# Row maxima of an attention stage: how they reach the query rows as extra contraction rows

## The chip, the cores and the metric

The kernel runs on one core of one Trainium2 chip. The metric is the device time of the whole kernel in microseconds (us), the median of several runs. One execution was also recorded by the hardware profiler; all start times below are us from the start of its span. The engines are called PE (TensorE), DVE (VectorE), ACT (ScalarE), POOL (GpSimd) and SP (SyncE, which issues DMAs). PEld is PE's loading of weights. "L1268" is line 1268 of the kernel before.

## The reference, cut to what matters

One layer of a hybrid encoder on 1024 tokens of width 1024 in float32: RMS norm, one combined projection, attention with 8 heads beside a convolution branch, gates, an output projection, and a mixture of 32 experts. The change touches the attention alone:

```python
# q, k: (1024, 8 heads, 96), v: (1024, 8 heads, 64); tokens are grouped in chunks of 64
s = einsum('bqhd,bkhd->bhqk', q, k) * scale
mask = key_chunk <= query_chunk          # a query sees its own chunk and all earlier ones
p = softmax(where(mask, s, -inf), axis=-1)
out = einsum('bhqk,bkhd->bqhd', p, v)
```

## The kernel before, in words

**Stages.** The projection units fill the first 340 us. The last of their epilogue and the opening of the attention lie at 340 to 374 us, the attention proper at 374 to 567 us, the branch projections up to about 654 us, the output projection with the router up to about 770 us, and the experts after that.

**The attention's items.** There are 16 items n, head h = n % 8 and group G = n // 8: group 0 holds queries 0 to 511 (4 key tiles of 128 keys), group 1 queries 512 to 1023 (8 key tiles). PE computes the scores twice. First it computes them with queries on partitions (`max_scores`, L1730), only so that DVE can take each query's maximum over its keys (L1218). Then it computes them transposed, with keys on partitions (`scores_T`, L1791 to L1793), so that ACT can take the exponential (`exps`, L908) and PE can multiply by the values (`pv`, L1804).

**How maximum and mask enter the transposed scores.** The query operand `qT` has 96 data rows and 12 further rows, and the key operand `kT` too (XK = 96 + 12 = 108 rows). Rows 96 to 103 carry the mask: a key column has -1e30 in the row of its own tile where the key lies in the tile's second chunk, and the query column has 1 in that row where the query lies in the tile's first chunk. Rows 104 to 107 subtract the maximum: the keys have four rows of ones, and the query columns have the negated maximum of query tile i in row 104 + i and zeros in the other three.

**The step in question, "mT".** DVE writes the negated maxima of an item as four columns of a small tile `nmax` [128 queries, 108] whose columns 96 to 103 are ones. PE transposes `nmax` into a PSUM bank (L1714, one transpose of 128 columns, output 108 x 128). DVE then multiplies rows 96 to 107 of that, repeated over the four query tiles, by a constant mask `own_tile` and writes the 12 x 512 result into `qT` (L1268):

```python
v.tensor_tensor(qT[t % 3][0][rows, :]..., M[rows, 0:P]...broadcast_to([XK - QK, GT, P]),
                own_tile[t // HEADS][rows, :, :], ALU.mult).then_inc(m_free[b], 1)
```

There are 16 such steps, mT(0) to mT(15). `scores_T` of an item waits for the semaphore `m_free` that this step increments.

**The order of the work.** Each engine's order is written out by hand. `OPENING` lists the work before the first transposed score (mT(0) is in it). Then, for each item n and key tile k, every engine walks the same list `slots(n, k)` of small jobs ("misc"): PE issues `scores_T(x + 2)`, the jobs, `pv(x)`; ACT issues `exps(x + 2)`, its part of the jobs and, at an item's last tile, two copies of sums and values out of PSUM (L941, L942); DVE does its part of the jobs and the reciprocals of the sums (L1352). In group 0 mT(n + 1) stands first in the slot k = 0; in group 1 it stands in the slot k = 2. The other jobs are the pieces of `max_scores` for item n + 2, the transpose of the queries (`qT`: PE L1709, ACT L845, DVE L1263), and in group 0 the preparation of tokens 512 to 1023 (q0, q1, kv0, kv1, kT0, kT1, ks). All jobs that need a PSUM bank take turns in two banks, and PE's next job in a bank waits for the `m_free` of the last one.

POOL fills the constants: `nmax`'s ones at the start (L608 to L610), `key_pad` and `own_tile` before the attention (L641 to L650). Every `qT` buffer gets its rows from 96 on from `own_tile` once (`mask_rows`, L671).

Of the kernel before, what the change touches and what calls it, by code (L numbers as in the profile page):

```python
# [26 lines left out]
ALU = mybir.AluOpType  # L27
ACT = mybir.ActivationFunctionType
AX = mybir.AxisListType

P = 128
D = 1024
T = 1024
NTILE = T // P
KD = D // P
HEADS, NOPE, ROPE, VD = 8, 64, 32, 64
QK = NOPE + ROPE
# [10 lines left out]
CHUNK = 64  # L48
# [13 lines left out]
TAPS_PER_UNIT = 7  # L62
LO_SPLIT = 5
LN_UNIT = 20
LN_SPLIT = (6, 11, 15, 19)
RUN = 4


def build(nc, x, positions, g_mix, w_in, g_q_lora, w_uq, g_kv_lora, w_ukv, g_qk_q, g_qk_k,
# [4 lines left out]
    base = (nc.sbuf_base + 127) // 128 * 128  # L74
# [11 lines left out]
    def small(name, shape, dt=F32):  # L86
        n = 2 if dt == BF16 else 4
        for s in shape[1:]:
            n *= s
        return place(name, shape, dt, room(n))  # L90
# [30 lines left out]
    qT = [[place(f"qT_{n}{r}", [P, CW], F32R, o + 2 * K * s) for s, n in enumerate(("hi", "lo"))] for r, o in enumerate(q_at)]  # L121
    qn = [place(f"qn{t}", [P, HEADS, QK], F32, o) for t, o in enumerate(
        (R2 + 56 * K, R2 + 8 * K, R2 + 11 * K, R3 + 29 * K, R6 + 12 * K, R6 + 16 * K, R2, R2 + 3 * K))]
    XK = QK + 12
    kn = [place(f"kn{i}", [P, HEADS, XK], F32, R2 + o) for i, o in enumerate((59 * K, 16 * K, 22 * K + 512, 26 * K))]
    sq2 = place("sq2", [P, HEADS, QK], F32, R2 + 19 * K + 512)
    pT = place("pT", [P, 3, CW], F32, R2 + 22 * K + 512)
# [40 lines left out]
    qd = place("qd", [P, NTILE, DOWN], F32, QDO)  # L168
# [33 lines left out]
    rs1 = small("rs1", [P, NTILE])  # L202
    ss3 = small("ss3", [P, 3, NTILE])
    ssh = small("ssh", [P, 4, 2, HEADS])
    key_pad = small("key_pad", [P, NTILE, 12])
    nmax_a = small("nmax_a", [P, 4])
    nmax = [small(f"nmax{i}", [P, XK]) for i in range(2)]
    wr = place("wr", [P, KD, NG + NE], F32, R6)
    br = place("br", [P, NG + NE], F32, R6 + 2 * K)
    lg = place("lg", [P, NTILE, NG], F32, R6 + 3 * K)  # L210
# [63 lines left out]
    with ctx:  # L274
# [117 lines left out]
        def piece_at(n, i):  # L392
            return GT * n + i if n < HEADS else GT * HEADS + 2 * GT * (n - HEADS) + i
# [192 lines left out]
        def _(pool):  # L586
# [3 lines left out]
            def link(ins):  # L590
                n[0] += 1
                ins.then_inc(pch, 1)
                pool.wait_ge(pch, n[0])
# [11 lines left out]
            g.memset(ab[:, NTILE, :], 0.0)  # L605
            g.memset(one_row[:, :], 1.0)
            g.memset(zero_i[:, :], 0)
            for i in range(2):  # L608
                link(g.memset(nmax[i][:, :], 0.0))
                g.memset(nmax[i][:, QK:QK + NTILE], 1.0)  # L610
            link(g.memset(before[:, :], 0.0))

            g.affine_select(out=before[:, :], in_=before[:, :], compare_op=ALU.is_ge, fill=1.0, base=0,
# [25 lines left out]
            pool.wait_ge(conv_done, NC)  # L639
            g.memset(vv[:, :, :, VD:2 * VD], 1.0)  # L640
            link(g.memset(key_pad[:, :, :], 0.0))  # L641
            link(g.memset(key_pad[:, :, NTILE:NTILE + 4], 1.0))
            for t in range(NTILE):
                link(g.memset(key_pad[CHUNK:P, t, t:t + 1], MASKED))
            for G in range(2):
                link(g.memset(own_tile[G][:, :, :], 0.0))
                link(g.affine_select(out=own_tile[G][:, :, 0:CHUNK], in_=own_tile[G][:, :, 0:CHUNK], compare_op=ALU.not_equal, fill=1.0,
                                     base=-(QK + GT * G), pattern=[[-1, 4], [0, CHUNK]], channel_multiplier=1))
                g.affine_select(out=own_tile[G][:, :, :], in_=own_tile[G][:, :, :], compare_op=ALU.not_equal, fill=1.0,
                                base=-(QK + NTILE), pattern=[[-1, 4], [0, P]], channel_multiplier=1).then_inc(pad_ok, 1)  # L650

            def q_norm(t):
                s2 = ssh[:, t % 4, :, :]
# [102 lines left out]
        def _(act):  # L756
# [49 lines left out]


            def misc(kind, t):
                if kind[:2] in ("mx", "mT", "qd", "kd", "ks"):
                    return  # L810
                b, nth = place_of[kind, t]
                M = pb[:, MISC_BANK[b], :]
                act.wait_ge(m_full[b], nth + 1)
                h = 4 * (kind[-1] == "1")
                if kind in ("q0", "q1"):
                    if (kind, t) == ("q0", GT + 2):
                        for i in range(2):
                            act.wait_ge(gate_out[i], 16 * KD)
                    a.activation(qn[t][:, h:h + 4, :], M[:, 0:4 * QK].rearrange("p (h c) -> p h c", h=4), ACT.Copy).then_inc(m_free[b], 1)
                    if kind == "q1":  # L820
                        b0, nth0 = place_of["q0", t]
                        act.wait_ge(m_free[b0], nth0 + 1)
                        act.wait_ge(m_free[b], nth + 1)
                        if t:
                            act.wait_ge(head_ss, sums_of(kind, t))
                        a.activation(sq2[:, :, :], qn[t][:, :, :], ACT.Square).then_inc(qk_sq, 1)
                if kind in ("kv0", "kv1"):
                    kv = M.rearrange("p (h c) -> p h c", h=4)
                    k = kn_of(t)
                    if t == 0:  # L830
                        act.wait_ge(pad_ok, 2)
                    a.activation(k[:, h:h + 4, 0:NOPE], kv[:, :, 0:NOPE], ACT.Copy)
                    a.activation(vv[:, t, h // 2:h // 2 + 2, :].rearrange("p a (s c) -> p a s c", s=3)[:, :, 0::2, :],
                                 kv[:, :, NOPE:].rearrange("p (a s) c -> p a s c", s=2), ACT.Copy).then_inc(m_free[b], 1)
                    if kind == "kv1":
                        b0, nth0 = place_of["kv0", t]
                        act.wait_ge(m_free[b0], nth0 + 1)
                        act.wait_ge(m_free[b], nth + 1)
                        act.wait_ge(head_ss, sums_of(kind, t))
                        a.activation(sq2[:, :, 0:NOPE], k[:, :, 0:NOPE], ACT.Square).then_inc(qk_sq, 1)  # L840
                if kind in ("kT0", "kT1"):
                    a.activation(kT[0][0:XK, h:h + 4, t * P:(t + 1) * P], M[0:XK, :].rearrange("p (h t) -> p h t", h=4),
                                 ACT.Copy, scale=vcol[0:XK, V_NK:V_NK + 1]).then_inc(qk_hi, 1)
                if kind == "qT":
                    a.activation(qT[t % 3][0][0:QK, :], M[0:QK, :], ACT.Copy, scale=vcol[0:QK, V_NQ:V_NQ + 1]).then_inc(qk_hi, 1)  # L845

# [242 lines left out]
        def _(dve):  # L1089
# [120 lines left out]
            def misc(kind, t):  # L1210
                if kind[:2] == "mx":
                    i, G = int(kind[2]), t // HEADS
                    y = piece_at(t, i)
                    tile = i // 2 if G else i
                    w = CW if G and i % 2 == 0 else (tile + 1) * P
                    to = nmax_a[:, tile:tile + 1] if G and i % 2 == 0 else nmax[t % 2][:, QK + NTILE + tile:QK + NTILE + tile + 1]
                    dve.wait_ge(sc_ok, y + 1)
                    v.tensor_reduce(out=to, in_=pb[:, 2 * (y % 2), 0:w], axis=AX.X, op=ALU.max, negate=True).then_inc(mx_ok, 1)  # L1218
                    if G and i == 2 * GT - 1:
                        dve.wait_ge(mx_ok, y + 1)  # L1220
                        m = nmax[t % 2][:, QK + NTILE:XK]
                        v.tensor_tensor(m, m, nmax_a[:, :], ALU.min).then_inc(mxc_ok, 1)
                        dve.wait_ge(mxc_ok, t - HEADS + 1)
                    return
                s2 = ssh[:, t % 4, :, :]
                if kind == "ks":
                    k = kn_of(t)
                    if t == 0:
                        dve.wait_ge(tab_ok, 1)
                    dve.wait_ge(head_rs, t + 1)  # L1230
                    v.tensor_tensor(k[:, :, 0:NOPE], k[:, :, 0:NOPE], s2[:, 1, :].unsqueeze(2).broadcast_to([P, HEADS, NOPE]), ALU.mult)
                    v.tensor_copy(k[:, :, QK:XK], key_pad[:, t:t + 1, :].broadcast_to([P, HEADS, 12]))
                    v.tensor_tensor(k[:, :, NOPE:QK], krr[:, t:t + 1, :].broadcast_to([P, HEADS, ROPE]),
                                    s2[:, 1, :].unsqueeze(2).broadcast_to([P, HEADS, ROPE]), ALU.mult).then_inc(k_ok, 1)
                    return
# [24 lines left out]
                if kind == "qT":  # L1260
# [1 line left out]
                    hi, lo = qT[t % 3]  # L1262
                    v.scalar_tensor_tensor(out=lo[0:QK, :], in0=M[0:QK, :], scalar=vcol[0:QK, V_NQ:V_NQ + 1], in1=hi[0:QK, :].bitcast(F32),  # L1263
                                           op0=ALU.mult, op1=ALU.subtract).then_inc(m_free[b], 1)
                if kind == "mT":
                    rows = slice(QK, XK)
                    dve.wait_ge(m_full[b], nth + 1)
                    v.tensor_tensor(qT[t % 3][0][rows, :].rearrange("p (i t) -> p i t", i=GT), M[rows, 0:P].unsqueeze(1).broadcast_to([XK - QK, GT, P]),  # L1268
                                    own_tile[t // HEADS][rows, :, :], ALU.mult).then_inc(m_free[b], 1)


            unit_lo(0)
# [343 lines left out]
        def _(pe):  # L1616
# [53 lines left out]
            def misc(kind, t):  # L1670
# [39 lines left out]
                if kind == "mT":  # L1710
                    pe.wait_ge(mx_ok, piece_at(t + 1, 0))
                    if t >= HEADS:
                        pe.wait_ge(mxc_ok, t - HEADS + 1)
                    i = t_.transpose(M[0:XK, 0:P], nmax[t % 2][:, :], ident[:, :])  # L1714
                i.then_inc(m_full[b], 1)

            def max_scores(n, i):
# [314 lines left out]
```

## Time and profile before

| | us |
|---|---|
| runs shown: median (lowest, highest) of 3 | 1154.52 (1152.56, 1154.81) |
| the profiled execution's own time | 1160.95 |
| its span, first to last instruction | 1158.9 |
| PE busy in the span | 1084.1 (94%) |
| DVE busy | 863.4 (74%) |
| ACT busy | 580.6 (50%) |
| POOL busy | 326.7 (28%) |

The mean granted clock of TensorE over the span is 0.981 of full speed. The chain of waits that ended last is PE for 46% of the span, DVE for 6%, DMA for 6% and ACT for 2%. In the timelines a line gives the start of a group of instructions, the time from the first one's start to the last one's end, engine, line, operation, output and inputs, shapes and the count; in brackets stands the idle time of the engine just before, and what ended it. Matmuls overlap: the distance between two starts is what one costs PE, its own duration is longer.

### The profile page before, as it was taken

What the parts mean: (1) busy time and instruction counts of PE and PEld (TensorE: products, weight loads), DVE (VectorE), ACT (ScalarE), POOL (GpSimd) and SP (SyncE); (2) the same over time, 40 slices, a digit from 0 to 9 for tenths busy, and PEclk for the clock granted to TensorE, in tenths of its full rate; (3) what the DMA queues carried; (4) which work ended last, traced back from release to release, by engine and by line L of the source; (5) the groups of instructions that cost most, each with busy time, mean ns of one, the idle gap of its engine ahead of it and who ended that gap; (6) DMA issues with size and microseconds to landing.
All of it is one profiled execution on the core that took longest, in us unless ns stands there. A gap on an engine that the chain in (4) does not pass through costs nothing.

```text
span 1158.9 us, 15310 instructions
## 1 busy us (share of the span) xinstructions
PE 1084.1 (94%) x5117; PEld 872.7 (75%) x5117; DVE 863.4 (74%) x1095; ACT 580.6 (50%) x738; POOL 326.7 (28%) x323
## 2 busy tenths in 40 slices
PE   6999999999998887999999999988999999998896
PEld 6988888888764555666688888877788888886684
DVE  5438999998547567667456666676999999997894
ACT  5531211221547553445423222224888888887883
POOL 4010000002084450000000000012477777763653
PEclk8999999999999998999999999998999999999998
DMA  6021222333110001000592245465999989988972
GB/s 247 1 55 36 54 84 87 101 104 96 64 37 18 1 0 37 1 1 1 167 312 66 61 176 187 182 232 183 330 358 338 313 322 309 325 303 294 331 243 33
DMA packets 99108, 176.47 MB, mean 152 GB/s; under 512 B 12364, under 2 KB 62711, under 8 KB 99063
## 3 DMA queue, kind: packets, MB, share of 16 engines
q1 hardware_dynamic: 86262, 150.69, 37.6%
q0 software_dynamic: 10432, 16.81, 6.1%
q10 hardware_dynamic: 2368, 8.41, 1.8%
q8 instruction: 24, 0.39, 0.1%
q14 instruction: 22, 0.17, 0.1%
HBM read 161.18 MB, written 35.65 MB: 170 GB/s over the span
## 4 chain that ended last, share of the span: by engine, by line
PE 46%; DVE 6%; DMA 6%; ACT 2%; issue 1%; SPq 1%; ACTq 0%; POOL 0%; DVEq 0%; POOLq 0%
PE pb L1621 11%; PE pb L1623 11%; PE pb L1622 11%; PE pb L1804 4%; DMA wed_raw<-in_w_e_down 4%; PE pb L1949 2%; DMA wgu_raw<-in_w_e_up 2%; PE pb L1867 1%; PE pb L1792 1%; PE pb L1793 1%; PE pb L1791 1%; PE pb L1730 1%; ACT wgu_hi L1011 1%; DVE prob_sums L1352 1%; PE pb L1858 1%
## 5 line engine op out<-in xcount | busy, mean ns | idle before, releaser
L1546 DVE TENSOR_TENSOR wgu_lo<-wgu_raw,wgu_hi 128x2048 fp32r<-128x2048 f32 x72 | 164.9, 2292 | 32.1 <-ACT wgu_hi L1011 30.2
L1161 DVE SCALAR_TENSOR_TENSOR cv<-up,dwc,cv 128x1024 f32<-128x1024 f32 x120 | 154.1, 1284 | 3.7
L1621 PE MATMUL pb<-hT_hi,ws_hi 128*128 128x512 f32 x384 | 155.0, 404 | 1.7 <-ACT lnr L889 1.6
L1011 ACT ACTIVATE wgu_hi<-wgu_raw 128x2048 fp32r (+1 forms) x72 | 137.9, 1916 | 25.8 <-issue 10.7
L1623 PE MATMUL pb<-hT_hi,ws_lo 128*128 128x512 f32 x384 | 149.8, 390 | 0.0
L1622 PE MATMUL pb<-hT_lo,ws_hi 128*128 128x512 f32 x384 | 149.7, 390 | 0.0
L1621 PE MATMUL pb<-wgu_hi,hgT_hi 128*128 128x512 f32 x288 | 116.7, 405 | 5.2 <-DVE hgT_lo L1550 5.2
L1623 PE MATMUL pb<-wgu_hi,hgT_lo 128*128 128x512 f32 x288 | 112.9, 392 | 0.0
L1622 PE MATMUL pb<-wgu_lo,hgT_hi 128*128 128x512 f32 x288 | 112.7, 391 | 0.0
L733 POOL DMA_INDIRECT out<-yb,rcol x36 | 71.0, 1973 | 99.3 <-PE pb L1949 44.0
L625 POOL TENSOR_SCALAR rs<-ss 128x1 f32<-128x1 f32 x16 | 5.3, 330 | 311.0 <-ACT h2T L971 294.6
L1578 DVE TENSOR_TENSOR wed_lo<-wed_raw,wed_hi 128x1024 fp32r<-128x1024 f32 x70 | 82.4, 1218 | 6.8 <-ACT wed_hi L1020 6.8
L1621 PEld LDWEIGHTS pb<-hT_hi,ws_hi 128*128 128x128 f32 x384 | 72.3, 188 | 19.2 <-issue 3.5
L1622 PEld LDWEIGHTS pb<-hT_lo,ws_hi 128*128 128x128 f32 x384 | 72.3, 188 | 16.6 <-issue 1.5
L1623 PEld LDWEIGHTS pb<-hT_hi,ws_lo 128*128 128x128 f32 x384 | 72.2, 188 | 15.2
L908 ACT ACTIVATE pT<-pb 128x512 f32<-128x512 f32 (+1 forms) x96 | 46.6, 489 | 68.2 <-PE pb L1793 67.9
L1020 ACT ACTIVATE wed_hi<-wed_raw 128x1024 fp32r x70 | 70.4, 1054 | 19.7 <-PE pb L1623 9.9
L1804 PE MATMUL pb<-pT,vv 128*128 128x512 f32 (+1 forms) x192 | 79.9, 499 | 0.0
L805 ACT ACTIVATE ws_hi<-ws_raw 128x1024 fp32r<-128x1024 f32 x32 | 33.8, 1059 | 80.1 <-PE pb L1623 47.8
L857 ACT ACTIVATE gring<-pb,vcol 128x1024 f32<-128x1024 f32 x16 | 17.9, 1118 | 107.8 <-PE pb L1623 107.8
L715 POOL TENSOR_TENSOR icol<-stok,zero_i 128x1 int32<-128x1 int32 x34 | 65.7, 1934 | 17.0 <-PE pb L1949 17.0
L1621 PEld LDWEIGHTS pb<-wgu_hi,hgT_hi 128*128 128x128 f32 x288 | 54.3, 188 | 19.8 <-issue 8.9
(329 smaller groups left out, 2535.2 us busy)
## 6 DMA issues: line engine op xcount, KB each, us to landing
wgu_raw<-in_w_e_gate SPq DMA_DIRECT2D x32, 1024.0 KB, 7.5
wgu_raw<-in_w_e_up SPq DMA_DIRECT2D x32, 1024.0 KB, 17.8
wed_raw<-in_w_e_down SPq DMA_DIRECT2D x32, 1024.0 KB, 20.0
ws_raw<-in_w_in SPq DMA_DIRECT2D x24, 512.0 KB, 3.7
gates_kept<-gring ACTq DMA_DIRECT2D x16, 512.0 KB, 2.6
gates<-gates_kept SPq DMA_DIRECT2D x16, 512.0 KB, 7.4
xs<-in_x SPq DMA_DIRECT2D x8, 512.0 KB, 8.5
wout<-in_w_out SPq DMA_DIRECT2D x1, 4096.0 KB, 14.4
```

The source lines that it names most:

```text
L715: g.tensor_tensor(icol[b][:, :], stok[:, bass.ds(count - 1, 1)], zero_i[:, :], ALU.add).then_inc(ic_ok, 1)
L733: g.indirect_dma_start(out=out[0], out_offset=bass.IndirectOffsetOnAxis(ap=rcol[b][:, 0:1].bitcast(U32), axis=0), in_=yb[b][:, :], in_offs ...
L908: a.activation(pT[:, x % 3, c0:CW], pb[:, 4 + x % 2, c0:CW], ACT.Exp).then_inc(ex_ok, 1)
L1011: a.activation(wgu_hi[q % 2][:, :, ks, :], raw, ACT.Copy).then_inc(gu_hi, 1)
L1020: a.activation((end_hi if end else wed_hi)[:, h, :], wed_raw[:, bass.ds((e + (DSLOTS - 1)) % DSLOTS, 1), h, :].rearrange("p o f -> p (o f) ...
L1161: i = v.scalar_tensor_tensor(out=cv[:, c, :], in0=src, scalar=w, in1=cv[:, c, :], op0=ALU.mult, op1=ALU.add)
L1546: v.tensor_tensor(wgu_lo[q % 2][:, :, ks, :], wgu_raw[:, bass.ds((e + (SLOTS - 1)) % SLOTS, 1), :, ks, :].rearrange("p o g k f -> p (o g) ...
L1578: v.tensor_tensor((end_lo if end else wed_lo)[:, h, :], wed_raw[:, bass.ds((e + (DSLOTS - 1)) % DSLOTS, 1), h, :].rearrange("p o f -> p (o ...
L1621: t_.matmul(out, w(0), m(0), start=start, stop=False)
L1622: t_.matmul(out, w(0), m(1), start=False, stop=False)
L1623: return t_.matmul(out, w(1), m(0), start=False, stop=stop)
L1804: t_.matmul(pb[:, VALUE_BANK[n % 2], c0:CW], vv[:, k, h // 2, VD * (h % 2):VD * (h % 2) + 2 * VD], pT[:, x % 3, c0:CW], start=(k == 0), st ...
```

## The change

`nmax` becomes one tile [128, 2 groups, 2 buffers, 4 query tiles, 9 columns]. Columns 0 to 7 of a query tile's nine are the mask, constants that POOL writes once: 1 in the first 64 partitions in the column of that tile of that group. Column 8 is the tile's negated maximum, which DVE writes. PE multiplies each of the four [128, 9] blocks with the identity, an ordinary matmul and not the transpose form, into the four 128-column parts of rows 96 to 104 of the PSUM bank. ACT copies these 9 x 512 values into `qT`, where DVE multiplied. The keys need one row of ones in place of four, so XK goes from 108 to 105 rows, and the tiles and copies of that width shrink with it.

```diff
-    XK = QK + 12
+    XK = QK + NTILE + 1
...
-    key_pad = small("key_pad", [P, NTILE, 12])
+    key_pad = small("key_pad", [P, NTILE, XK - QK])
-    nmax = [small(f"nmax{i}", [P, XK]) for i in range(2)]
+    nmax = small("nmax", [P, 2, 2, GTILE, XK - QK])
...  POOL, at the start
-            for i in range(2):
-                link(g.memset(nmax[i][:, :], 0.0))
-                g.memset(nmax[i][:, QK:QK + NTILE], 1.0)
+            link(g.memset(nmax[:, :, :, :, :], 0.0))
+            for G in range(2):
+                for i in range(GT):
+                    g.memset(nmax[0:CHUNK, G, :, i, GT * G + i:GT * G + i + 1], 1.0)
...  POOL, before the attention
-            link(g.memset(key_pad[:, :, NTILE:NTILE + 4], 1.0))
+            link(g.memset(key_pad[:, :, NTILE:NTILE + 1], 1.0))
...
-                                base=-(QK + NTILE), pattern=[[-1, 4], [0, P]], channel_multiplier=1).then_inc(pad_ok, 1)
+                                base=-(QK + NTILE), pattern=[[0, 4], [0, P]], channel_multiplier=1).then_inc(pad_ok, 1)
...  ACT, misc
-                if kind[:2] in ("mx", "mT", "qd", "kd", "ks"):
+                if kind[:2] in ("mx", "qd", "kd", "ks"):
...
+                if kind == "mT":
+                    act.wait_ge(mx_ok, piece_at(t + 1, 0))
+                    a.activation(qT[t % 3][0][QK:XK, :], M[QK:XK, :], ACT.Copy).then_inc(m_free[b], 1)
...  DVE, misc
-                    to = nmax_a[:, tile:tile + 1] if G and i % 2 == 0 else nmax[t % 2][:, QK + NTILE + tile:QK + NTILE + tile + 1]
+                    to = nmax_a[:, tile:tile + 1] if G and i % 2 == 0 else nmax[:, G, t % 2, tile, NTILE:NTILE + 1]
...
-                        m = nmax[t % 2][:, QK + NTILE:XK]
+                        m = nmax[:, G, t % 2, :, NTILE]
...
-                    v.tensor_copy(k[:, :, QK:XK], key_pad[:, t:t + 1, :].broadcast_to([P, HEADS, 12]))
+                    v.tensor_copy(k[:, :, QK:XK], key_pad[:, t:t + 1, :].broadcast_to([P, HEADS, XK - QK]))
...
-                if kind == "mT":
-                    rows = slice(QK, XK)
-                    dve.wait_ge(m_full[b], nth + 1)
-                    v.tensor_tensor(qT[t % 3][0][rows, :].rearrange("p (i t) -> p i t", i=GT), M[rows, 0:P].unsqueeze(1).broadcast_to([XK - QK, GT, P]),
-                                    own_tile[t // HEADS][rows, :, :], ALU.mult).then_inc(m_free[b], 1)
...  PE, misc
-                    i = t_.transpose(M[0:XK, 0:P], nmax[t % 2][:, :], ident[:, :])
+                    for j in range(GT):
+                        i = t_.matmul(M[QK:XK, j * P:(j + 1) * P], nmax[:, t // HEADS, t % 2, j, :], ident[:, :], start=True, stop=True)
```

## Rows read from the trace of the kernel before

**Rows 1.** Windows; columns: stretch, length, busy time per engine, granted clock, DMA.
```profile
420.00:440.00 20.00, 15.17 (x67) 10.08 (x65) 13.31 (x23) 10.88 (x22) 7.48 (x9) 0.88 0.00 1
440.00:455.00 15.00, 12.91 (x55) 9.51 (x54) 10.38 (x17) 5.92 (x11) 0.61 (x1) 0.81 0.25 70
...
475.00:495.00 20.00, 20.00 (x87) 14.03 (x87) 12.81 (x22) 10.21 (x19) 0.00 (x0) 1.00 0.00 1
```
**Rows 2.** Groups of instructions by shape, 366 to 566 us; busy, mean ns.
```profile
L1268 DVE TENSOR_TENSOR qT_hi<-pb,own_tile 12x512 fp32r<-12x512 f32 x16 | 11.2, 697 | 6.5 <-PE pb L1714 6.2
...
L941 ACT ACTIVATE prob_sums<-pb 64x512 f32<-64x512 f32 x16 | 9.5, 592 | 2.8 <-PE pb L1804 2.5
...
L1804 PE MATMUL pb<-pT,vv 128*128 128x128 f32 x32 | 6.2, 274 | 0.0
...
L1714 PE MATMUL pb<-ident,nmax 128*108 128x128 f32 x16 | 4.4, 275 | 1.2 <-DVE nmax L1218 0.6 <-DVE nmax L1222 0.5
```
**Rows 3.** Chain that ended last, 431 to 480 us; start, us, what.
```profile
436.97 0.70 DVE qT_hi L1268
...
446.27 0.70 DVE qT_hi L1268
...
457.71 0.70 DVE qT_hi L1268
...
470.58 0.11 PE pb L1714
...
476.62 0.44 PE pb L1709 x4
...
478.67 0.22 PE pb L1804 x2
```
**Rows 4.** Timeline of PE at 23 us, where small transposes stand between large work.
```profile
23.91 0.32 PE L1645 MATMUL pb<-ident,dwr 124*128 124x124 f32 x1
24.16 0.22 PE L1646 MATMUL pb<-ident,posf 8*128 8x8 f32 x1
24.32 1.09 PE L1633 MATMUL pb<-ident,xs 128*128 128x128 f32 x8
```
**Rows 5.** Timeline of PE, 378 to 462 us: group 0.
```profile
378.34 0.39 PE L1791 MATMUL pb<-qT_hi,kT_hi 108*128 108x256 f32 x1 [2.14 <-ACT pT L908]
...
389.29 1.12 PE L1700 MATMUL pb<-wukv,qdT 128*128 128x512 f32 x2 [2.01 <-DVE qT_lo L1263]
...
415.56 0.47 PE L1791 MATMUL pb<-qT_hi,kT_hi 108*128 108x512 f32 x1 [0.21 <-DVE qT_hi L1268]
...
424.78 0.82 PE L1705 MATMUL pb<-ident,kn 128*108 128x128 f32 x4 [1.55 <-DVE qT_lo L1263]
...
438.99 1.07 PE L1705 MATMUL pb<-ident,kn 128*108 128x128 f32 x4 [2.36 <-DVE kn L1233]
...
448.81 0.58 PE L1730 MATMUL pb<-kT_hi,qT_hi 104*128 104x512 f32 x1 [1.89 <-DVE nmax_a L1218]
...
451.75 0.82 PE L1730 MATMUL pb<-kT_hi,qT_hi 104*128 104x256 f32 x2
...
460.00 0.47 PE L1730 MATMUL pb<-kT_hi,qT_hi 104*128 104x512 f32 x1 [1.97 <-DVE nmax_a L1218]
...
461.65 0.51 PE L1730 MATMUL pb<-kT_hi,qT_hi 104*128 104x256 f32 x2
```
**Rows 6.** Timeline of ACT at 425 us.
```profile
424.91 0.38 ACT L908 ACTIVATE pT<-pb 128x256 f32<-128x256 f32 x1
425.63 0.69 ACT L842 ACTIVATE kT_hi<-pb,vcol 108x512 fp32r<-108x512 f32 x1 [0.34 <-PE pb L1705]
```
**Rows 7.** Windows of the same columns, finer.
```profile
426.00:428.00 2.00, 2.00 (x3) 0.68 (x3) 1.61 (x2) 0.70 (x3) 1.84 (x3) 0.50 0.00 0
```
**Rows 8.** Timeline of POOL at the start.
```profile
1.68 0.60 POOL L602 MEMSET invf<- 128x1 f32 x16
...
5.76 0.19 POOL L625 TENSOR_SCALAR rs<-ss 128x1 f32<-128x1 f32 x1 [1.20 <-ACT sqj L769]
```

More of the change, by code:

```diff
@@ L64 @@
 LN_UNIT = 20
+GTILE = 4
 LN_SPLIT = (6, 11, 15, 19)
```

## The prediction

> **What bounds the kernel now.** I read the busy windows of the attention first. In group 0 (to about 468 us) PE has idle time: 15.17 us busy of 20, then 12.91 of 15, and the granted clock is 0.88 and 0.81, so part of the time TensorE runs at 1.2 instead of 2.4 GHz. In group 1 PE is busy 20.00 us of 20 at clock 1.00, with DVE at 12.8 and ACT at 10.2 [rows 1]. So the two groups have different limits. The chain of waits says the same: from 431 to 460 us it goes through DVE again and again, the mask multiply L1268 among it three times, and from 468 us it is a row of PE instructions end to end, with the transpose L1714 itself in it [rows 3]. PE's timeline then gives the length of each stall in group 0 and who ended it [rows 5]. An edit that takes from DVE and gives to PE can thus win in group 0 and must lose in group 1.
>
> **What DVE gives up.** L1268 is 16 times 0.70 us, 11.2 us of busy time, and DVE sat 6.2 us in front of it waiting for PE [rows 2]. Only what stands on the path counts. In group 1 DVE's queue is not what PE waits for: nothing. In group 0 the instruction is on the chain at 436.97, 446.27 and 457.71 us [rows 3], steps mT(6) to mT(8); each is followed by a PE stall of 2.36, 1.89 and 1.97 us that ends with a DVE instruction queued behind it [rows 5], so each gives 0.7. At 415.56 us, mT(4), a transposed score waits 0.21 us for L1268 itself [rows 5] and later maxima come up to 0.7 earlier; I take 0.5. At mT(1) to mT(3) and mT(5) the stall behind the step hangs on a chain through ACT (a copy or a sum of squares) that L1268 doesn't delay: nothing. Sum: -2.6 us; bounds -0.6 (0.2 each at three places) and -5.6 (all eight of group 0).
>
> **What PE gets.** Out goes one transpose, 0.11 us in the chain. In come four ordinary float32 matmuls with 128 moving columns. The trace shows what such a one costs: L1804 with 128 columns is two instructions and 0.22 us, while four transposes are one instruction each and 0.44 us together [rows 3]. Only nine columns of weights don't help, since it is the moving columns that are streamed. Four times 0.22 less 0.11 is 0.77 us more per step at full clock. To that comes a price for small tiles between large ones. At 23.91 us a transpose of 124 columns is followed by the next start only after 0.25 us, and at 24.16 us one of 8 columns after 0.16 us [rows 4], where 124 columns should take 0.11 and 8 about 0.01: 0.14 to 0.15 us too much each time the shape changes. The new matmuls write partitions 96 to 104 only, the neighbours write whole tiles, so there are two such changes per step; I take 0.25 for both. Together 1.0 us per step. Bounds: 0.33 (one pass per matmul, as in a transpose) and 1.07; no gain is possible, because four passes replace one.
>
> The Trainium skill has a rule on this ("TensorEngine Tiling (Array Packing)", Key Properties): changing the tiling mode drains TensorE, and its restrictions say that column tiling excludes the transpose mode for float32 inputs. By that rule there would be two drains per step and no cheap form of the four products, which the 0.15 us of [rows 4] agrees with; by it the step would be at 1.07 instead of 1.0 us.
>
> Where does PE's extra time land? In group 1 PE has no idle time, and mT(9) to mT(15) lie there: seven times 1.0. The few DVE stalls late in group 1 start from an exponential that waits for PE, so they move along and absorb nothing. mT(0) in the opening and mT(1) at 378.80 us come before no stall but ones that hang on PE's own later results (the 2.14 us at 378.34 wait for ACT, whose input PE made after mT(0) [rows 5]): two more. That makes 9 x 1.0 = +9.0 us. The other seven steps of group 0 stand ahead of stalls that other engines end (2.01, 1.55, 2.36, 1.89, 1.97 us [rows 5], and two slightly shorter than 1.0), which swallow the 1.0 us.
>
> **What ACT gets.** Sixteen copies of 9 x 512 from PSUM; the nearest row is 64 x 512, 0.592 us [rows 2]. Behind the copy on ACT stands the exponential of the next tile, whose input PE finishes more than 1 us after the step, since a product with the values comes between: hidden. The exceptions are item ends in group 0, where ACT also makes its two copies of 0.59 us. At 424.91 us comes an exponential of 0.38 and at 425.63 the key copy L842 [rows 6]; the new copy goes between and ends near 425.9, and PE's next product waits for the bank that it frees. Until now L1268 freed it: DVE began it as PE's stall ended at 424.78 [rows 5], so it was done by 425.5: +0.4 to 0.5 us, taken as 0.45. If the cover were gone everywhere, ACT would cost 16 x 0.59 = 9.4; I take 0.45 and keep up to 2. The copy adds no wait of weight: ACT waits for PE's step, and every later input of ACT is behind that step in PE's order.
>
> **The clock.** Of 420 to 455 us, 20 x 0.12 x 2 + 15 x 0.19 x 2 = 10.5 us ran at half clock [rows 1], in three stretches (one of them in [rows 7]), each right behind one of the stalls of 1.55, 2.36 and 1.89 us; stalls of 2.14, 2.01 and 1.97 us had none [rows 5]. One such stretch costs 1.3 us: the same work from one L1730 to the next takes 2.94 us from 448.81 and 1.65 us from 460.00 [rows 5]. All three: 3.9 us by this, at most 10.5 / 2 = 5.2; I take 4.5. With PE 1.0 us longer and DVE 0.7 us shorter these stalls shrink to some 0.5, 0.7 and 0.2 us. I expect two of the three stretches to stay at 2.4 GHz: -3.0 us; bounds 0 and -5.2.
>
> **Nothing.** 105 for 108 contraction rows: the streamed columns stay. POOL: nine memsets for four at the start, five more at 0.60 / 16 = 0.04 us, before an idle time of 1.20 us [rows 8]. Narrower key copies on DVE: under 0.1 us each.
>
> **The sum.** +9.0 + 0.45 - 2.6 - 3.0 = +3.9 us, on the profiled execution 1160.95 (span 1158.9 and 2.05 around it), so 1164.8. The profiled execution is 6.4 us above the median of the runs, and I carry the difference over: 1154.52 + 3.9 = 1158.4 us. Everything after the attention waits for it through PE and moves as a whole.
>
> **Rivals.**
> - *Repaid in group 0.* The small-tile changes cost nothing (0.77 per step: 9 x 0.77 = 6.9) and all half-clock stretches go: 6.9 + 0.45 - 2.6 - 4.5 = +0.3, 1154.8 us. For it: the stalls do shrink. Against: [rows 4].
> - *Faster: nine-column products are cheap.* If each of the four streams in one pass, a step adds 0.33 us, and it decides from there: 9 x 0.33 + 0.45 - 2.6 - 4.5 = -3.7, 1150.8 us. The change of sign lies near 0.74 us per step with the clock fully back. For it: the transposes of 128 columns cost 0.11. Against: L1804 of the same 128 columns is two instructions.
> - *Dearer: nothing comes back.* The step is 1.07, the stalls move to other places and the clock falls as often as before: 9 x 1.07 + 0.45 - 2.6 = +7.5; without DVE's gains too, +10.1: 1162 to 1164.6 us. For it: three stalls as long had no effect on the clock, so its rule is not in the gap alone.
> - *The change does nothing*, because ACT takes over DVE's part unseen and PE's extra time is absorbed: only in group 0 is there room for that; I count it in the first rival.
>
> **Chances.** Forecast 0.50, repaid 0.20, faster 0.13, dearer 0.17. A measurement tells 0.2%, 2.3 us, from no change. Slower by more: 0.17 and nearly all of the forecast, 0.62. Within: the first rival and a rest of the forecast, 0.23. Faster: 0.15. Range 1152.5 to 1163.5.
>
> **What would show it.** Right: eight PE instructions of 128 moving columns per step, and 1.0 us more from the step's first start to the next product's; from mT(9) to mT(15) six steps, so 6 us more between their starts; ACT's copy near 0.59; the DVE-ended stalls behind mT(5) to mT(8) under 1 us; a clock above 0.88 and 0.81 in group 0. Wrong: four instructions per step, or group 1 no longer than before (then PE was not its limit), or half-clock stretches as before or at new places.

## The result and the profile after

Over 15 runs each, the changed kernel took a median of 1162.6 us (1158.5 to 1167.2) and the kernel before 1156.5 us (1151.2 to 1165.1), side by side on the same chip. The ratio is 1.0045, with a 95% interval of 1.0026 to 1.0064: 5.2 us slower, between 3.0 and 7.4. The forecast was 3.9 us slower. In the profiled execution of the changed kernel the span is 1160.5 us, the mean granted clock 0.985 and its own time 1162.49 us. The page shows PE busy for 1096.7 us in 5229 instructions (before 1084.1 us in 5117; 112 more, seven for each of 16 steps), DVE 848.6 us (863.4) and ACT 590.0 us (580.6).

The busy windows of the kernel after, columns as in [rows 1]:

```profile
380.00:387.00 7.00, 7.00 (x27) 4.75 (x25) 2.63 (x6) 1.47 (x3) 3.70 (x5) 0.76 0.00 0
...
420.00:440.00 20.00, 17.08 (x90) 11.87 (x89) 13.04 (x25) 12.62 (x25) 7.48 (x9) 1.00 0.00 1
440.00:455.00 15.00, 13.25 (x74) 9.94 (x74) 12.24 (x20) 9.04 (x17) 1.22 (x2) 1.00 0.25 71
...
475.00:495.00 20.00, 20.00 (x90) 13.58 (x89) 10.86 (x19) 10.52 (x20) 0.00 (x0) 1.00 0.00 1
```

The two stretches of group 0 that had a clock of 0.88 and 0.81 [rows 1] now have 1.00, and a new lower stretch, 0.76, stands at 380 us. In group 1 PE was full before and is full now.

The groups of instructions, 366 to 570 us, columns as in [rows 2]:

```profile
L1223 DVE TENSOR_REDUCE nmax_a<-pb 128x1 f32<-128x512 f32 x32 | 22.0, 686 | 19.0 <-PE pb L1731 18.9
...
L1715 PE MATMUL pb<-ident,nmax 128*9 128x128 f32 x128 | 16.7, 273 | 1.2 <-DVE nmax L1223 0.7 <-DVE nmax L1227 0.6
L848 ACT ACTIVATE qT_hi<-pb 9x512 fp32r<-9x512 f32 x16 | 9.4, 590 | 3.9 <-PE pb L1715 3.7
```

A step is now 8 PE instructions (128 in 16 steps), as forecast: four products, two passes each. ACT's copy of nine partitions takes 590 ns, as long as its copy of 64 [rows 2]. The first row is DVE's reduction: it stood idle 19.0 us in all, 18.9 of it for PE; the same group of before stood idle 6.1 us.

The chain that ended last, 440 to 486 us, columns as in [rows 3]:

```profile
444.17 0.97 PE pb L1715 x8
...
455.97 0.29 PE pb L1731
456.29 0.70 DVE nmax_a L1223
457.13 0.47 PE pb L1731
...
467.75 0.97 PE pb L1715 x8
468.72 0.43 PE pb L1731
```

The step's own 0.97 us stands where the transpose's 0.11 us stood, in both groups; the mask multiply is gone from it.

PE's timeline of the kernel after, columns as in [rows 5]:

```profile
379.25 0.28 PE L1794 MATMUL pb<-qT_hi,kT_lo 96*128 96x256 f32 x1
379.46 1.04 PE L1715 MATMUL pb<-ident,nmax 128*9 128x128 f32 x8
380.43 1.22 PE L1805 MATMUL pb<-pT,vv 128*128 128x512 f32 x1
...
426.87 0.69 PE L1705 MATMUL pb<-ident,kn 128*105 128x128 f32 x4 [0.67 <-DVE qT_lo L1268]
428.06 1.12 PE L1700 MATMUL pb<-wukv,qdT 128*128 128x512 f32 x2 [0.50 <-ACT qT_hi L848]
...
439.33 0.66 PE L1705 MATMUL pb<-ident,kn 128*105 128x128 f32 x4 [0.80 <-DVE kn L1238]
447.64 0.47 PE L1731 MATMUL pb<-kT_hi,qT_hi 104*128 104x512 f32 x1 [0.82 <-DVE nmax_a L1223]
...
457.13 0.47 PE L1731 MATMUL pb<-kT_hi,qT_hi 104*128 104x512 f32 x1 [0.82 <-DVE nmax_a L1223]
...
507.99 0.40 PE L1794 MATMUL pb<-qT_hi,kT_lo 96*128 96x512 f32 x1
508.31 1.04 PE L1715 MATMUL pb<-ident,nmax 128*9 128x128 f32 x8
509.29 0.50 PE L1731 MATMUL pb<-kT_hi,qT_hi 104*128 104x512 f32 x1
509.62 1.02 PE L1805 MATMUL pb<-pT,vv 128*128 128x512 f32 x2
```

The stalls of 1.55, 2.36, 1.89 and 1.97 us [rows 5] are 0.67, 0.80, 0.82 and 0.82 us here. At 428.06 us PE waits 0.50 us for ACT's new copy: the one place where the forecast let it show.

To find where the time went, I take the start of each step mT(i) on PE as a mark, and the first product of the branches as the last one, and compare the distances between marks. The last column says what the experiments below make of the difference. "Half clock" is a granted clock of 1.2 instead of 2.4 GHz.

| from, to | before, us | after, us | difference | of what |
|---|---|---|---|---|
| mT(0), mT(1) | 7.92 | 8.82 | +0.90 | PE's step |
| mT(1), mT(2) | 8.21 | 10.88 | +2.67 | PE's step 1.05, new half-clock stretch 1.62 |
| mT(2), mT(4) | 24.51 | 24.22 | -0.29 | DVE |
| mT(4), mT(5) | 11.43 | 10.60 | -0.83 | DVE |
| mT(5), mT(6) | 11.85 | 10.72 | -1.13 | ACT +0.4, clock -1.5 |
| mT(6), mT(7) | 10.36 | 8.22 | -2.14 | DVE -0.7, clock -1.4 |
| mT(7), mT(8) | 11.02 | 9.50 | -1.52 | DVE -0.1, clock -1.4 |
| mT(8), mT(9) | 14.24 | 14.08 | -0.16 | DVE |
| mT(9), mT(15) | 76.71 | 83.05 | +6.34 | PE's step, 6 x 1.057 |
| mT(15), branches | 15.50 | 16.49 | +0.99 | PE's step |
| all | 191.75 | 196.58 | +4.83 | |

Group 0 as a whole gains 2.5 us and group 1 loses 7.3. Of the 4.8 us only 1.6 are left in the spans of these two executions (1158.9 and 1160.5), because the execution of before ran 572 to 580 us at a granted clock of 0.79 and that of after at 1.00, and lost more time behind the attention than after did, 3.0 us in all. The timed difference of 5.2 us agrees with the attention, not with the two spans. The agreement can't be pressed: another execution of before's group 0 code took 4 us longer (under the experiments).

### The profile page after: what moved, and what is told of

Its sections match the earlier page's. It is cut to its first block, busy times and chain, and to the rows that moved or that the text cites. A ratio compares the mean times of both kernels' runs of the same rounds, so it can differ in the third digit from the quotient of the medians.

```text
span 1160.5 us, 15555 instructions
## 1 busy us (share of the span) xinstructions
PE 1096.7 (95%) x5229; PEld 880.2 (76%) x5229; DVE 848.6 (73%) x1079; ACT 590.0 (51%) x754; POOL 327.6 (28%) x328
## 4 chain that ended last, share of the span: by engine, by line
PE 44%; DMA 8%; DVE 5%; ACT 2%; issue 1%; SPq 1%; ACTq 0%; POOL 0%; DVEq 0%; POOLq 0%
PE pb L1621 10%; PE pb L1623 10%; PE pb L1622 10%; DMA wed_raw<-in_w_e_down 7%; PE pb L1805 4%; PE pb L1950 2%; PE pb L1868 1%; PE pb L1731 1%; PE pb L1794 1%; PE pb L1793 1%; PE pb L1792 1%; PE pb L1715 1%; DVE prob_sums L1352 1%; PE pb L1859 1%; PE pb L1937 1%
```

## The experiments

The theory was the forecast's: PE's longer step is lost in group 1 and in the opening, while group 0 gives something back through DVE and the clock. The rivals were that the cost is the small output tile and not the products, that the products themselves are cheap, and that DVE's relief does nothing. The ratios are to the kernel before in the same session; 1156.5, 1158.0 and 1157.0 us are its medians in three sessions.

**PE's extra work alone, group 0.** The kernel before, with the four small products put ahead of its transpose. The transpose overwrites them and DVE still multiplies.

```diff
+                    if t < HEADS:
+                        for j in range(GT):
+                            t_.matmul(M[QK:XK, j * P:(j + 1) * P], nmax[t % 2][:, QK:XK], ident[:, :], start=True, stop=True)
                     i = t_.transpose(M[0:XK, 0:P], nmax[t % 2][:, :], ident[:, :])
```

> The kernel before, and in the steps of group 0 (mT(0) to mT(7)) PE also makes the changed kernel's four small ordinary products (written into the same bank and then overwritten by the transpose); DVE keeps its mask multiply, ACT gets nothing. Theory (PE's time is absorbed in group 0 but for the first two steps, and fills gaps in which the clock would fall): +2.1 us for mT(0) and mT(1), 0 to -3 for the clock, so 0.998 to 1.002 of before; the starts of mT(9) and mT(15) stay 76.7 us apart. Rival (PE's extra time costs wherever it stands): 8 x 1.05 = +8.4 us, 1.007.

1156.64 us, ratio 0.9989 (0.9962 to 1.0015): no difference. The distances behind mT(2), mT(3) and mT(4) are 11.64, 12.85 and 11.44 us, those of before to 0.02 us: the steps vanish in stalls that other engines end. At mT(0) they don't: 8.93 us against 7.92; and at mT(1) it takes 10.92 us against 8.21, with a half-clock stretch as in after. These are the two steps that the forecast counted in group 0. Where the execution of before ran at half clock, its second profile (below) gives the comparison: 10.27 us against 10.36 behind mT(5), 9.82 against 9.61 behind mT(7). Behind mT(6) and mT(8) one of the two ran at half clock in part, and the step can't be read off. From 400 to 455 us this kernel ran at a clock of 1.00 throughout, though DVE is not relieved in it; from 455 to 475 us it had 0.91. So the unchanged median does not mean that all eight steps cost nothing: two of them show their 1.0 us, and less half-clock time from 400 to 455 us stands against it.

**The same in group 1.** The edit with `t >= HEADS`.

> The same addition, but only in the steps of group 1 (mT(8) to mT(15)); nothing else of the change. Theory (group 1 pays in full): seven steps of 1.05, +7.4 us, 1.006 of before; mT(9) to mT(15) 83.0 us apart instead of 76.7. Rival (the time is lost through ACT's new copy and not through PE): no ACT copy here, so 1.000 and 76.7 us. The clock in group 0 stays as in the kernel before (0.88 and 0.81 from 420 to 455 us) if it is PE's longer and DVE's shorter work in group 0 that raised it.

1166.27 us, ratio 1.0063 (1.0044 to 1.0083), +7.3 us. From mT(9) to mT(15) it takes 83.50 us against 76.71: 1.13 us per step, nothing absorbed. That is the whole loss of the change and more. The same eight instructions per step leave the total as it was in one group and cost 7 us in the other.

In group 0 this kernel has the code of before, so its profile is also one more execution of that code. It was expected to have the clock of before there (0.88 and 0.81 from 420 to 455 us). It has half-clock stretches in the same places, and another one at 376 us:

```profile
376.00:380.00 4.00, 4.00 (x12) 2.69 (x12) 1.77 (x4) 0.66 (x2) 3.68 (x6) 0.50 0.02 4
...
420.00:440.00 20.00, 15.09 (x65) 9.81 (x63) 13.45 (x23) 11.04 (x23) 7.46 (x9) 0.90 0.00 1
440.00:455.00 15.00, 12.93 (x48) 9.78 (x48) 10.13 (x16) 5.36 (x11) 0.61 (x1) 0.73 0.24 70
```

From mT(0) to mT(8) it takes 89.30 us, and before 85.30: 4.0 us between two executions of the same instructions.

**The four products with full-width output.** The blocks are 105 columns wide (96 of zeros ahead), so the products write partitions 0 to 104, as the neighbours do. POOL writes the mask columns before the attention and again for group 1, and in group 1 DVE joins the maxima with four instructions and not one. The cut shows PE's line alone.

```diff
-                        i = t_.matmul(M[QK:XK, j * P:(j + 1) * P], nmax[:, t // HEADS, t % 2, j, :], ident[:, :], start=True, stop=True)
+                        i = t_.matmul(M[0:XK, j * P:(j + 1) * P], nmax[t % 2][j][:, :], ident[:, :], start=True, stop=True)
```

> The changed kernel, but the four blocks are 105 columns wide (96 zero columns ahead of the nine), so the products write partitions 0 to 104 and not 96 to 104: the same eight instructions of 128 moving columns without a change of tile shape. Theory (passes 0.77, shape changes 0.25 to 0.30 per step): mT(9) to mT(15) 76.7 + 6 x 0.77 = 81.3 us apart, and 9 x 0.28 = 2.5 us faster than the changed kernel: +2.7 us on before, 1.002. Rival (the small tile is the price, the passes hide behind other work): near 78 us apart.

1160.15 us, ratio 1.0012 (0.9988 to 1.0037). PE's timeline of this kernel at the same step as the last rows shown of after, mT(12):

```profile
508.21 0.40 PE L1810 MATMUL pb<-qT_hi,kT_lo 96*128 96x512 f32 x1
508.44 1.04 PE L1731 MATMUL pb<-ident,nm_a 128*105 128x128 f32 x8
509.24 0.47 PE L1747 MATMUL pb<-kT_hi,qT_hi 104*128 104x512 f32 x1
509.55 1.02 PE L1821 MATMUL pb<-pT,vv 128*128 128x512 f32 x2
```

From the last score product to the first of the eight it is 0.23 us here and 0.32 in after; from there to the next neighbour 0.80 and 0.98. The eight instructions are the same, so going into the small tile and out again costs about 0.3 us. Loading the blocks as weights is not what makes the small tile dear: it takes 90 ns there and 185 ns with the full width. The rows are of after, then of this kernel:

```profile
L1715 PEld LDWEIGHTS pb<-ident,nmax 128*9 128x9 f32 x128 | 10.4, 90 | 7.3 <-issue 4.7
```

```profile
L1731 PEld LDWEIGHTS pb<-ident,nm_a 128*105 128x105 f32 x64 | 8.5, 185 | 3.0 <-issue 2.7
```

Over six steps the distance is 81.20 us, 0.75 us per step more than before, against 1.057 in after: 0.31 us for the two changes.

The forecast cited "TensorEngine Tiling (Array Packing)", Key Properties, of the Trainium skill, by which a change of tiling mode drains TensorE. The 0.31 us measured here is what such a drain would look like; no run shows that it is one. The step came out at 1.06 us, which is the 1.07 that the forecast worked out from [rows 4] and put beside the rule, and not the 1.0 that I took.

**Full-width transposes.** The same blocks, in the transpose form.

```diff
+                        i = t_.transpose(M[0:XK, j * P:(j + 1) * P], nmax[t % 2][j][:, :], ident[:, :])
```

> As the run with full-width products, but the four blocks are transposed in the transpose form: four instructions of one pass, 0.44 us per step, no change of tile shape; ACT copies, DVE is relieved. Theory: 0.33 us more per step than before, mT(9) to mT(15) 78.7 us apart; 9 x 0.33 + 0.45 - 2.6 and 0 to -4.5 for the clock: -3.7 to +0.8 us, 0.997 to 1.001 of before. Rival (ACT's copy and its place in the order cost as much as PE's passes): slower than before, 1.003 or more, with the distance of mT(9) to mT(15) clearly over 79 us.

1156.63 us, ratio 0.9974 (0.9953 to 0.9994): 3.0 us faster than the kernel before, 0.7 to 5.4. PE's timeline at mT(12):

```profile
498.99 0.40 PE L1810 MATMUL pb<-qT_hi,kT_lo 96*128 96x512 f32 x1
499.22 0.60 PE L1731 MATMUL pb<-ident,nm_a 128*105 128x128 f32 x4
499.58 0.48 PE L1747 MATMUL pb<-kT_hi,qT_hi 104*128 104x512 f32 x1
499.90 1.02 PE L1821 MATMUL pb<-pT,vv 128*128 128x512 f32 x2
```

Four instructions in place of eight. From mT(9) to mT(15) it takes 78.70 us, 0.33 us per step more than before, which is the forecast's lower bound of 3 x 0.11. The step's price, and with it the sign of the change, is thus a matter of the form of the four products: two passes and a small tile 1.06, two passes 0.75, one pass 0.33 us.

**DVE copies in place of ACT.** The changed kernel, but its nine rows are copied by DVE, which gives DVE its 0.70 us back and takes ACT's copy out.

```diff
-                    a.activation(qT[t % 3][0][QK:XK, :], M[QK:XK, :], ACT.Copy).then_inc(m_free[b], 1)
+                    v.tensor_copy(qT[t % 3][0][QK:XK, :], M[QK:XK, :]).then_inc(m_free[b], 1)
```

> The changed kernel, but DVE and not ACT copies the 9 x 512 values from PSUM into the query rows: PE's products as in the changed kernel, DVE again with an instruction of 0.6 to 0.7 us in its old place. Theory (DVE's relief is worth 2.6 us in group 0, ACT's copy costs 0.45 there): 2.2 us slower than the changed kernel, 1.0064 of before; in the timeline the stalls of PE that DVE ends behind mT(6) to mT(8) are 0.7 us longer than in the changed kernel; mT(9) to mT(15) 83.0 us apart as there. Rival (DVE's relief is worth nothing, PE's longer step alone filled the gaps and held the clock): no slower than the changed kernel, 1.0045.

1164.88 us, ratio 1.0067 (1.0041 to 1.0093), where the change itself has 1.0045 (1.0026 to 1.0064); the intervals overlap, so the times alone don't settle it. The traces do. First the copy's group, then PE's timeline of this kernel:

```profile
L1269 DVE CAST qT_hi<-pb 9x512 fp32r<-9x512 f32 x16 | 11.2, 697 | 16.0 <-PE pb L1715 15.6
```

```profile
440.51 0.66 PE L1705 MATMUL pb<-ident,kn 128*105 128x128 f32 x4 [1.52 <-DVE kn L1235]
...
448.89 0.48 PE L1731 MATMUL pb<-kT_hi,qT_hi 104*128 104x512 f32 x1 [0.89 <-DVE nmax_a L1220]
...
458.68 0.48 PE L1731 MATMUL pb<-kT_hi,qT_hi 104*128 104x512 f32 x1 [1.10 <-DVE nmax_a L1220]
```

The copy is as dear as the multiply, 697 ns. The stall at mT(6) grows from 0.80 to 1.52 us, by the 0.7 us of the instruction; those at mT(7) and mT(8) grow only from 0.82 to 0.89 and 1.10. This kernel and after are both at full clock from 400 to 475 us, so their distances give DVE's and ACT's terms by themselves, step by step. Ahead of mT(2) this kernel had more half-clock time (mT(0) to mT(2) 22.28 us against 19.70 in after), so nothing can be read off there; from mT(3) to mT(4) the two are equal to 0.03 us.

| interval | DVE copies | ACT copies (after) | ACT's gain |
|---|---|---|---|
| mT(2), mT(3) | 11.66 | 11.36 | 0.30 |
| mT(4), mT(5) | 11.44 | 10.60 | 0.84 |
| mT(5), mT(6) | 10.27 | 10.72 | -0.45 |
| mT(6), mT(7) | 8.96 | 8.22 | 0.74 |
| mT(7), mT(8) | 9.58 | 9.50 | 0.08 |
| mT(8), mT(9) | 14.33 | 14.08 | 0.25 |

**The change in group 0 only.** Group 1 has the transpose and the mask multiply of before; the blocks are 12 columns wide for it.

```diff
+                    if t < HEADS:
+                        for j in range(GT):
+                            i = t_.matmul(M[QK:XK, j * P:(j + 1) * P], nmax0[:, t % 2, j, :], ident[:, :], start=True, stop=True)
+                    else:
+                        i = t_.transpose(M[0:XK, 0:P], nmax[t % 2][:, :], ident[:, :])
```

> The whole change in group 0 only (small products on PE, copy on ACT, no DVE multiply), with 12 columns per block instead of 9; group 1 as in the kernel before. Theory: what group 1 paid falls away, 7 x 1.06 = 7.4 us off the changed kernel's +5.2: -2.2 us, 0.998 of before; by the prediction's own terms 2.0 + 0.45 - 2.6 - 3.0 = -3.1, 0.997; mT(9) to mT(15) 76.7 us apart. Rival (DVE's relief also helps in group 1, or the part in group 0 brings nothing): 1.001 or more.

1155.36 us, ratio 0.9995 (0.9971 to 1.0019). The interval holds a gain of 3 us and a loss of 2, so the time decides nothing between a group 0 that pays and one that doesn't. What it does say is where the loss of the change lay: with group 1 as before it is gone. In the trace mT(0) to mT(9) takes 96.92 us (before 99.54, after 97.04) and mT(9) to mT(15) 76.64 (before 76.71). It had no half-clock stretch at 380 us, but one behind mT(8), 0.93 from 440 to 455 us.

**Full-width transposes in group 0 only.**

```diff
+                    for j in range(GT if t < HEADS else 1):
+                        i = t_.transpose(M[0:XK, j * P:(j + 1) * P], nmax[t % 2][j][:, :], ident[:, :])
```

> Four full-width transposes per step and ACT's copy in group 0, one transpose and DVE's multiply as before in group 1. Theory: the gain of the run with full-width transposes (0.9974 of before) less what it still paid in group 1, 7 x 0.33 = 2.3 us: -5.3 us, 0.9954 of before; mT(9) to mT(15) 76.7 us apart. Rival (that gain came from group 1, where DVE had less to do, or was chance): 0.9974 or nearer to 1.

1153.6 us, ratio 0.9970 (0.9942 to 0.9998). It is faster than before, but the expected 0.9954 and the full version's 0.9974 both lie in the interval, so the time doesn't decide between them: the 6 x 0.33 us that group 1 should give back do come back (76.75 us from mT(9) to mT(15)), while group 0 took 96.52 us in this execution against 93.38 in the other. The windows of this kernel show by what:

```profile
366.00:372.00 6.00, 6.00 (x19) 3.68 (x18) 1.48 (x4) 2.08 (x4) 0.00 (x0) 0.72 0.23 90
...
376.00:380.00 4.00, 3.62 (x13) 2.58 (x14) 0.00 (x0) 1.68 (x4) 3.60 (x7) 0.61 0.00 0
```

**Both kernels profiled once more.** The half-clock stretches are a term of the sum, so I looked at whether they belong to the kernel or to the execution. Nothing is edited; one run each.

> The kernel before, unchanged, profiled once more, to see which of its half-clock stretches belong to the kernel and which to the execution. If the three stretches behind the stalls of 1.5 to 2.4 us in group 0 belong to the kernel: clock below 0.95 again in 420 to 440 and in 440 to 455 us. If they are chance: at least one of the two windows at 1.00. mT(9) to mT(15) 76.7 us apart in any case.

1156.18 us, span 1154.1. Windows of this second execution of before:

```profile
376.00:380.00 4.00, 3.67 (x14) 2.64 (x15) 1.23 (x3) 1.31 (x4) 3.60 (x7) 0.63 0.00 0
...
420.00:440.00 20.00, 15.07 (x69) 10.23 (x68) 14.31 (x25) 11.66 (x24) 7.48 (x9) 0.96 0.00 1
440.00:455.00 15.00, 12.01 (x60) 9.20 (x58) 12.39 (x20) 7.16 (x15) 1.22 (x2) 0.94 0.24 70
```

> The changed kernel, unchanged, profiled once more. If PE's longer steps keep the clock up in group 0: 0.97 or more in 400 to 455 us again. If the half-clock stretch at 380 to 387 us belongs to the change and not to the execution, the clock is below 0.95 in 380 to 400 us again. mT(9) to mT(15) 83.05 us apart in any case.

1161.08 us, span 1159.1. A window of this second execution of after:

```profile
420.00:440.00 20.00, 17.11 (x91) 11.90 (x89) 13.06 (x25) 12.83 (x26) 7.47 (x9) 1.00 0.00 1
```

The kernel before again had half-clock time where it had it, but less (0.96 and 0.94 for 0.88 and 0.81; neither the "below 0.95 in both" nor the "1.00 in one" that was expected), and some at 366 us (0.72 to 372 us) and at 376 us. The kernel after was again at 1.00 there, and again lower near 380 us (0.91 from 380 to 400 us in both its executions). All of the distances of after came back to 0.06 us. Those of before came back to 0.07 us except at mT(0), mT(1), mT(5) and mT(7), where the clock differs: 10.36 for 11.85 us at mT(5), 9.61 for 11.02 at mT(7), and 0.97 and 1.63 us longer at the first two. So the gain in 420 to 455 us is real, and its size is the execution's: 4.3 us in the profiled execution of before, about 1.5 in the second. In the whole of group 0 the two executions of before differ by only 0.23 us (99.54 and 99.31), since what one lost late the other lost early. That they agree is chance: from mT(0) to mT(8) they take 85.30 and 85.07 us, and the run with the extra work in group 1 only, the same code there, 89.30.

What keeps the clock up can be read from all the profiles. The three executions in which the steps mT(0) to mT(7) are those of before have 0.88, 0.90 and 0.96 from 420 to 440 us, and 0.81, 0.73 and 0.94 from 440 to 455. The two kernels that lengthen PE's step there and leave DVE its instruction (PE's extra work alone in group 0, and DVE copies) have 1.00 in both. So PE's longer step is enough, without DVE's relief. The granted clock of all timed runs gives a check that doesn't hang on single executions. In one session its mean was 0.980 for before (33 runs), 0.983 with PE's extra work in group 0 and 0.980 with the same in group 1, 0.985 and 0.984 for the two full-width versions. In the other it was 0.981 for before (29 runs), 0.984 for DVE copies, but 0.982 for both versions that change group 0 only, so that there the gain doesn't show.

No run has the transpose form with its output in partitions 96 to 104, or a one-pass float32r product there. Whether the four products could be cheap in the small tile stays open.

## Why the prediction was right, and where it was off

**What bounds each group: right.** PE full in group 1, other engines at the end of group 0's stalls. The pair of kernels with PE's extra work alone shows it directly: +7.3 us in one group, no difference in the other, where only mT(0) and mT(1) show the step and less half-clock time stands against it. It was read from two windows and a chain before anything was built [rows 1, 3].

**PE's step.** Forecast 1.0 us, at nine steps: +9.0. Measured 1.057 in group 1, 0.90 at mT(0) and 1.05 at mT(1); with 0.99 behind mT(15) it makes 0.90 + 1.05 + 6.34 + 0.99 = +9.3. The passes were forecast at 0.77 and came to 0.75. The tile change was forecast at 0.25 for both ways from two small transposes [rows 4] and came to 0.31: half of that reading, 0.14 to 0.15 each, doubled, would have been 0.29, and I had rounded down.

**ACT.** Forecast +0.45 at mT(5) and nothing elsewhere. The distance from mT(5) to mT(6) is 0.45 us longer with ACT's copy than with DVE's, and PE waits there 0.50 us for it. The copy's 0.59 us and its cover at the other steps held as well.

**DVE: the place right, the size partly wrong.** Forecast -2.6: 0.7 at mT(6), mT(7) and mT(8), 0.5 at mT(4). Measured 0.74, 0.08, 0.25 and 0.84, and 0.30 at mT(2), where I had counted nothing: -2.2 with all five. The sum came out close because two errors offset each other. The step that failed is "each is followed by a PE stall ... that ends with a DVE instruction queued behind it, so each gives 0.7". At mT(7) and mT(8) the stall of 1.9 us (forecast to shrink to 0.2 at mT(7), measured 0.82) shrank by PE's own 1.0 first, and what was left of it could shrink little more: in the chain after, PE's product at 455.97 us feeds the reduction at 456.29, which takes 0.70 us, and PE goes on behind it at 457.13. DVE was waiting for PE there, and with the mask multiply back on DVE that wait only fills up (stalls of 0.89 and 1.10 for 0.82). I had let PE's extra 1.0 us vanish in those stalls and also took DVE's 0.7 there, which counts the same slack twice.

**The clock.** Forecast -3.0: two of three half-clock stretches gone. All three went (-1.5, -1.4 and -1.4, together -4.3), and a new one came at 380 us, in front of which stands the 2.14 us stall for ACT at 378.9 us, unchanged. It costs 1.62 us: 10.88 from mT(1) to mT(2), where the change in group 0 only had 9.26 at clock 1.00. Net -2.7. The forecast had named half-clock stretches at new places only as what would make it wrong; that there would be one, at this size, was not foreseen. That the net came so near -3.0 is therefore luck: two of three gone was forecast, and three of three gone and a new one measured. Nor is the new stretch tied to the change: both executions of after have it, as has the kernel with PE's extra work alone, but the version with the change in group 0 only has not.

**The sum.** +9.3 + 0.45 - 2.2 - 2.7 = +4.9, against +4.83 between the marks and +5.2 (3.0 to 7.4) in the timed runs; forecast +3.9. Since most of these terms were read from the same distances, the first agreement is bookkeeping. The second is in part luck, since group 0 of before has been seen to take 4 us more (89.30 for 85.30 us); which clock term the timed runs have on average is not known. The missing 0.9 to 1.3 us are the tile change, the over-counted DVE term and 0.3 us of clock.

**The rivals.** *Nine-column products are cheap* fell: eight instructions per step. It named the right lever, though: in the one-pass form the step costs its 0.33 us and the kernel is 3.0 us faster than before, near the -3.7 that this rival gave. *Repaid in group 0* fell by the step's price, 1.057 us for its 0.77, in a group where nothing repays; that all three old stretches go, its other half, did happen. *Dearer* had the step's 1.07 right and the clock wrong. The absolute time, 1158.4 us, came out 4.2 us too low: 2.0 of it is the base, 1154.52 as a median of three runs where 15 gave 1156.5, and the rest is the change, 6.1 us between the two medians. With that base corrected *dearer* would have had 1164.0 to 1166.6, so that the measured 1162.6 lies in its stated 1162 to 1164.6 only by the low base.

## What to carry to other kernels

Read for each stage which engine has no idle time, and price an edit there and not by the busy shares of the whole kernel: the same eight PE instructions left the total unchanged in one group and cost 7.3 us in the other. For a small float32 move through PE, count the moving columns and the passes, and keep the output tile of the shape of its neighbours: the four transposes of 105 columns, mostly zeros, cost 0.33 us per step, the four products of the same width 0.75, and the four products of nine columns 1.06. Where a stall is to absorb one engine's extra work and another engine's relief is to shorten it, it can do only one of them.

## What the runs showed of the hardware that was not expected

- A plain copy of 9 x 512 from PSUM on DVE takes 697 ns, as long as the multiply of 12 x 512 by a mask [rows 2]; on ACT it takes 590 ns for 9, 12 and (592) 64 partitions.
- The half-clock stretches move between executions of one and the same kernel: 0.88 or 0.96 from 420 to 440 us in before, and 1.00 or 0.63 near 376 us. Here is the start of the first execution of before, and of the second:

```profile
20.00:30.00 10.00, 10.00 (x52) 9.30 (x51) 5.09 (x10) 3.64 (x10) 3.98 (x7) 0.88 0.41 106
```

```profile
20.00:30.00 10.00, 10.00 (x60) 9.39 (x60) 6.11 (x11) 5.17 (x17) 3.94 (x7) 1.00 0.41 107
```

- PE is busy all of these 10 us both times. The eleven profiled executions are of two kinds, though the code ahead of the attention is nearly the same in all. In five (both of after, one of before, two experiments) the clock was 0.88 to 0.91 from 20 to 30 us and 0.96 from 300 to 340 us, and mT(0) starts at 370.4 to 370.9 us. In six (the second of before, five experiments) it was 1.00 in both, and mT(0) starts at 367.4 to 367.9 us. These 3 us are part of the scatter of the runs, 1151 to 1165 us, and one profile against one other can't resolve a change of 3 us by its span; distances between marks can.
- Of stalls of like length (2.14, 2.01, 1.55, 2.36, 1.89 and 1.97 us [rows 5]) three were followed by a half-clock stretch in one execution. In the second the ones at mT(5) and mT(7) were not, but the 2.14 us one, which ended at 376.32 us there, was. In a third execution of this code, the run with the extra work in group 1 only, there were half-clock stretches behind the same three stalls again, and one near 376 us. What decides it was not found.
